# The first pair of a feed-forward layer takes both down units ahead of P4, and three of five layers make its T4 by an accumulating transfer

## What is computed

```python
def swiglu(x, w_gu, w_down):
    gate, up = jnp.split(x @ w_gu, 2, axis=-1)     # w_gu: 1024 x 5632
    return (jax.nn.silu(gate) * up) @ w_down       # w_down: 2816 x 1024
...
h = h + 0.5 * rmsnorm_2(swiglu(rmsnorm_2(h, g[0]), ffn_w_gu[l, 0], ffn_w_down[l, 0]), g[1])
```

## Time and profile before

| | us |
|---|---|
| median of 3 runs | 1264.8 (1263.88 to 1267.02) |
| the profiled execution | 1265.15 |
| its span, first to last instruction | 1263.4 |
| PE busy | 1249.7 (99%) |
| DVE busy | 1042.2 (82%) |
| ACT busy | 804.7 (64%) |
| POOL busy | 197.8 (16%) |

### The profile page before, as it was taken

How to read it: one execution, slowest core, us unless ns; L and a number is a source line. 1 busy time by engine, 2 the same in 40 slices (tenths; PEclk the granted TensorE clock), 3 DMA queues, 4 the chain that set the end, 5 groups by cost and what they waited for, 6 DMA issues and landing times.

```text
span 1263.4 us, 15541 instructions
## 1 busy us (share of the span) xinstructions
PE 1249.7 (99%) x5897; PEld 1029.2 (81%) x5897; DVE 1042.2 (82%) x1036; ACT 804.7 (64%) x988; POOL 197.8 (16%) x224
## 2 busy tenths in 40 slices
PE   9999999999999999999999999999999999999998
PEld 7888888888888888888878888888888877788886
DVE  6766689999799996767899997999977568899984
ACT  6674576666576664645666664766656467766662
POOL 6142130110001100202301101211001003301100
PEclk9999999999999999999999999999999999999999
DMA  9537498997649955568989978389745535999931
GB/s 335 175 101 229 128 327 251 267 273 250 199 147 253 272 172 187 194 223 213 334 242 247 265 248 260 123 240 274 219 167 179 180 125 170 321 287 263 266 133 44
DMA packets 143003, 277.32 MB, mean 220 GB/s; under 512 B 8993, under 2 KB 39897, under 8 KB 142929
## 3 DMA queue, kind: packets, MB, share of 16 engines
q1 hardware_dynamic: 120192, 229.67, 52.1%
q0 software_dynamic: 22288, 45.54, 19.7%
q10 hardware_dynamic: 448, 1.12, 0.2%
HBM read 275.24 MB, written 1.05 MB: 219 GB/s over the span
## 4 chain that ended last, share of the span: by engine, by line
PE 83%; DVE 8%; DMA 3%; issue 3%; ACT 2%; POOL 0%; SPq 0%; DVEq 0%; POOLq 0%; ACTq 0%
PE B L2115 15%; PE B L2117 15%; PE B L2116 15%; PE B L2571 7%; PE B L2573 7%; PE B L2572 7%; DVE w_lo L1366 5%; PE T L2115 3%; PE T L2117 3%; PE T L2116 3%; DMA Z<-in_ffn_w_gu 2%; DVE VD L1385 1%; ACT w_hi L1084 1%; PE T L2595 1%; DMA VD<-in_ffn_w_gu 1%
## 5 line engine op out<-in xcount | busy, mean ns | idle before, releaser
L1366 DVE TENSOR_TENSOR w_lo<-w_raw,w_hi 128x2048 fp32r<-128x2048 f32 x129 | 296.5, 2300 | 87.3 <-ACT w_hi L769 87.0
L769 ACT ACTIVATE w_hi<-w_raw 128x2048 fp32r<-128x2048 f32 x129 | 247.2, 1919 | 102.2 <-PE B L2573 59.7
L2115 PE MATMUL B<-w_hi,xt_lo 128*128 128x512 f32 x652 | 259.8, 398 | 2.4 <-DVE nat L2029 0.6
L2117 PE MATMUL B<-w_hi,xt_hi 128*128 128x512 f32 x652 | 254.5, 390 | 0.0
L2116 PE MATMUL B<-w_lo,xt_hi 128*128 128x512 f32 x652 | 254.1, 390 | 0.0
L2571 PE MATMUL B<-w_hi,act_lo 128*128 128x512 f32 x440 | 172.8, 393 | 0.8 <-DVE w_lo L1366 0.6
L2573 PE MATMUL B<-w_hi,act_hi 128*128 128x512 f32 x440 | 171.5, 390 | 0.0
L2572 PE MATMUL B<-w_lo,act_hi 128*128 128x512 f32 x440 | 171.3, 389 | 0.0
L2115 PEld LDWEIGHTS B<-w_hi,xt_lo 128*128 128x128 f32 x652 | 122.5, 188 | 31.5 <-issue 4.4
L2117 PEld LDWEIGHTS B<-w_hi,xt_hi 128*128 128x128 f32 x652 | 122.4, 188 | 26.1
L2116 PEld LDWEIGHTS B<-w_lo,xt_hi 128*128 128x128 f32 x652 | 122.6, 188 | 23.3
(11 more groups left out here) (331 smaller groups left out, 2115.9 us busy)
## 6 DMA issues: line engine op xcount, KB each, us to landing
w_raw<-in_ffn_w_down SPq DMA_DIRECT2D x88, 512.0 KB, 5.8
Z<-in_ffn_w_gu SPq DMA_DIRECT2D x64, 512.0 KB, 8.2
w_raw<-in_ffn_w_gu SPq DMA_DIRECT2D x48, 512.0 KB, 5.3
nat<-in_ffn_w_gu SPq DMA_DIRECT2D x32, 512.0 KB, 7.9
QT<-in_ffn_w_gu SPq DMA_DIRECT2D x32, 512.0 KB, 7.0
Z<-in_ffn_w_gu POOLq DMA_DIRECT2D x32, 512.0 KB, 9.1
w_raw<-in_conv_w_in SPq DMA_DIRECT2D x24, 512.0 KB, 4.8
w_raw<-in_w_down SPq DMA_DIRECT2D x22, 512.0 KB, 6.6
```

Source lines behind the costliest of these rows:

```text
L769: act.activation(whi[home(u)][:, :], raw[slot][:, :], ACT.Copy).then_inc(w_hi, 1)
L1366: dve.tensor_tensor(wlo[home(u)][:, :], src, whi[home(u)][:, :].bitcast(F32), ALU.subtract).then_inc(w_lo, 1)
L2115: pe.matmul(bank[:, :], lo[:, k, x], whi[s][:, c], start=first, stop=False, skip_group_check=more)
L2117: return pe.matmul(bank[:, :], hi[:, k, x], whi[s][:, c], start=False, stop=last, skip_group_check=more)
```

## The change

- `FFN_OPS` in pair 0: D0, D1, P4 instead of D0, P4, D1, on all engines that walk it.
- T4.0 in f = 1, 3, 4 (`FIRST_T4`) is made by an accumulating transfer that POOL issues after P6.0's low half; DVE's sum goes, and SP's refill of B21 no longer waits for it. In f = 0, 2 DVE still makes it, now after D0's low half.
- `act_out(1)` has the second pair of activation buffers and moves from the end of pair 0 to behind P3.0, on ACT and DVE.
- Sum T4.3 moves on DVE from behind P6.3 to behind act_out(7), ahead of P2.3.
- In f = 2 the sums T1.2 and T1.3 move on DVE from ahead of the down unit Db to behind C11.
- In SP's queue in pair 0, B12 is refilled ahead of B21.

```diff
-FFN_OPS += [(_n, 0) for _n in ("P1", "P2", "P5", "P6", "P3", "P7")] + [("D0", 0), ("P4", 0), ("D1", 0)]
+FFN_OPS += [(_n, 0) for _n in ("P1", "P2", "P5", "P6", "P3", "P7", "D0", "D1", "P4")]
...
 ADDED_T4 = (1, 2)
+FIRST_T4 = (1, 3, 4)
+def added_t4(f):
+    return ((0,) if f in FIRST_T4 else ()) + ADDED_T4
 def sums_of(f):
-    return (((0, "T1"), (0, "T2")) if f % 2 else ()) + ((0, "T4"),) + SUMS
+    return (((0, "T1"), (0, "T2")) if f % 2 else ()) + (() if f in FIRST_T4 else ((0, "T4"),)) + SUMS
...
         def act_parts(d):
-            return (ahi1, alo1) if is_second(d) else (ahi, alo)
+            return (ahi1, alo1) if d == 1 or is_second(d) else (ahi, alo)
... SP
-                        if name == "B21" and p == 0:
+                        if name == "B21" and p == 0 and f not in FIRST_T4:
                             sp.wait_ge(t_ok, sums_ready(f, 0, "T4"))
                 next_block("B22", "P3", 0)
+                next_block("B12", "P7", 0)
                 next_block("B21", "P2", 0)
-                next_block("B12", "P7", 0)
... POOL, add_blocks
+                if p0 and 0 in added_t4(f):
+                    add_block("T4", f, 0, w_gu)
                 for p in range(p0, SQUARES):
                     add_block("T3", f, p, w_gu)
-                    if p in ADDED_T4:
+                    if p in added_t4(f):
                         add_block("T4", f, p, w_gu)
... ACT
                 def act_out(d):
-                    if d == 1:
-                        act.wait_ge(w_used, u0 + OP["D0", 0] + 1)
                 block("P3", 0)
+                act_out(1)
                 keep("P5", 0)
                 block("P7", 0)
                 keep("P6", 0)
                 weights("D0")
+                weights("D1")
                 block("P4", 0)
-                weights("D1")
-                act_out(1)
... DVE
                 block("P3", 0)
-                weight_sum("T4", f, 0)
+                act_out(1)
                 block("P7", 0)
                 weights("D0")
-                block("P4", 0)
+                if f not in FIRST_T4:
+                    weight_sum("T4", f, 0)
                 result("C22", 0)
                 weights("D1")
                 result("C12", 0)
+                block("P4", 0)
+                result("C11", 0)
                 weight_sum("T1", f, 1)
-                act_out(1)
-                result("C11", 0)
                 for p in range(1, SQUARES):
...
-                    if p not in ADDED_T4:
-                        weight_sum("T4", f, p)
                     block("P3", p)
                     block("P7", p)
                     act_out(2 * p)
                     weights("Da", p - 1)
                     act_out(2 * p + 1)
+                    if p not in added_t4(f):
+                        weight_sum("T4", f, p)
                     block("P2", p)
                     result("C22", p)
                     block("P4", p)
                     result("C12", p)
-                    if p + 1 < SQUARES:
+                    if p + 1 < SQUARES and f != 2:
                         weight_sum("T1", f, p + 1)
                     weights("Db", p - 1)
                     result("C11", p)
+                    if p + 1 < SQUARES and f == 2:
+                        weight_sum("T1", f, p + 1)
... PE
                         down("D0")
+                        down("D1")
                     pe.wait_ge(c_ok, m + 1)
                     block("P4", p)
                     if p:
                         down("Db", p - 1)
-                    else:
-                        down("D1")
```

More of the change, by code:

```diff
@@ L79, in t4_added @@
 def t4_added(f, p):
-    return 32 * (len(ADDED_T4) * f + ADDED_T4.index(p) + 1)
+    return 32 * (sum(len(added_t4(g)) for g in range(f)) + added_t4(f).index(p) + 1)
 def down_block(name, p):
@@ L1078, in block @@
                         act.wait_ge(*((t1_in, 32 * f + 64) if src == "T1" else (t2_in, 16 * f + 32)))
-                    elif src == "T4" and p in ADDED_T4:
+                    elif src == "T4" and p in added_t4(f):
                         act.wait_ge(t4_in, t4_added(f, p))
```

## The result

The changed kernel takes 1275.4 us, median of 6 runs (1274.08 to 1276.89), against 1264.9 for the kernel before beside it (1263.88 to 1267.02): ratio 1.0077, 95% interval 1.0067 to 1.0088. The forecast was 1265.3, no change; it is 10.6 us slower. The profiled execution took 1276.89, with a span of 1275.1 and a granted clock of 0.999.

What follows compares the result with a forecast made beforehand. PE, busy 1249.7 of 1263.4 us, was the bound, so only its stalls could move. Layers f=0 to 4 at +0.68, -0.81, +2.08, -0.71, -0.71 gave +0.53: median 1265.3, own range 1263.5 to 1267.5, over all cases 1261.5 to 1268.0.

Steps and rivals of the forecast that it cites:

- The stall at P7.0: PE in pair 0: a stall of 0.41 and restart of about 0.1 go, 0.53 saved.
- P3.3's: Stall after pair 3's transposes goes as T4.3 moves: gain 0.68 in f=1 and f=2, 0.18 in f=0, 3, 4.
- The stalls of D1 and Db.1 in f=2: PE in f=2: 0.38 + 0.12 at D1 and 0.58 + 0.16 with restart 0.15 at Db.1 both go.
- The 23.15 chain of f=0 and f=2: Pair 0, D0's high half to P6.1 with DVE's late sum: P6.1 late, +0.86 in f=0, +0.37 in f=2.
- T1 behind Db: f=2, pairs 2 and 3: DVE and ACT chain 17.56 against PE's 16.32, P6 late, +2.68 in all.
- T3's lateness: f=2, T3 issued later behind the moved T1: 0.3 per pair, bounds 0 and 2.4.
- rival C: T3 late in f=2 by the full 2.4 per pair: +4.2, 1269.5; decides over 10.5 us from issue; chance 0.07.
- the three signs by which I would be wrong: P6.1 stalls in f=3 or f=4, T4.0 takes over 11 us, or P5.1 does not stall in f=0.
- The added transfer: T4.0 in f=1, 3, 4 lands 9.96 after issue, hidden; 0.15 put on f=1 for B12, bounds 0 and 1.5.
- 0.5 of cover and 0.09 of spare: Pair 0: T4.0 lands 0.5 before P4.0's high half must start; DVE's chain reaches P6.1 with 0.09 left.
- rival D: T4.0 lands late in f=1, 3, 4, sliding all to P6.1: 1.8 each, +5.4, 1270.7; chance 0.05.
- the lock rule: DVE and POOL share ports under an exclusive lock, so T4.0's issue could stand behind one more DVE step of 2.28.

Runs made afterwards that it cites:

- e4: The kernel before with only the sum T4.3 moved on DVE from behind P6.3 to ahead of P2.3, all layers: 1262.6 us, ratio 0.9983.
- e10: e4 with SP's refill of B22 behind that of B12 in every pair: 1263.7 us, ratio 0.9987.
- e7: The kernel before, SP's plain transfers after T3.2 and T3.3 also waiting for C11 (2.53 behind, not 1.93): 1264.9 us, ratio 1.0.
- e2: The changed kernel with the refill of B22 in pair 0 issued behind that of B12: 1271.1 us, ratio 1.0046.
- e11: e6 with the refill of B22 behind that of B12 in every pair: 1260.4 us, ratio 0.9963.
- e6: The changed kernel with T4.0 by transfer in all layers, pair 0's B22 behind B12, T1 ahead of Db, T1.1 ahead of P4.0: 1264.5 us, ratio 1.0.
- e12: The changed kernel with the sum T1.1 on DVE ahead of P4.0's low half and C11: 1280.8 us, ratio 1.0126.

## Why the prediction was wrong

**Right.** The stall at P7.0 goes in all layers. P3.3's goes, and the move pays 2.4 (e4) for 1.9. The stalls of D1 and Db.1 in f=2 go too, but that proves nothing: e4 and e10 keep D1 and T1 at their old places and have neither stall in f=2 (e4 has 0.99 at Db.1 in f=1 instead), and e7 has none at D1 and 0.15 at Db.1. I read 0.38 and 0.74 as the kernel's, and they were that one execution's. The 23.15 chain of f=0 and f=2 gives stalls of 0.52 and 0.69 or 0.81 with the restart, as forecast. T1 behind Db: the stalls of P5 and P6 in pairs 2 and 3 add to 2.9 for 2.68, and T3's lateness to 0.8 for 0.6 (it landed in 11.9 and 12.0, past the 10.5 at which rival C decides, at a fifth of C's price). The rows for these, steps back to back, were enough. Two of the three signs by which I would be wrong came: P6.1 stalls in f=3, and T4.0 takes over 11 us.

**The step that failed: "The added transfer".** I took one row, 9.96, as T4.0's duration, on the argument that pair 1's transfer "has the same size". What it does not have is the same neighbour. In the earlier trace rows SP's next plain transfer is issued 2.40 behind; for the new one it is 1.98 in f=1 and 2.05 in f=3, as P3.0's low half follows P6.0's at once, and SP refills B22 on it. It measured 12.67 and 12.26, and 10.12 in f=4 at 2.17. With only 0.5 of cover and 0.09 of spare behind, that is rival D, which I gave 0.05: it names the place and the slide to P6.1, at 1.8 a layer. The runs give 2.2 in f=1 and 1.7 in f=3 and nothing in f=4. So D's place came true and its cause did not. The text gave as cause the lock rule of the Trainium skill's page "SBUF — State Buffer", section "SBUF: two separate sides"; against DVE steps with two inputs, as here, the rule asks for a GpSimd operation that reads SBUF, and no trace shows POOL's issue to be one. It is 2.49 long, no longer than in the kernel before (2.43 to 2.50), and starts 0.3 after P6.0's low half is written. e2 shows another cause, since the same issue beside the same DVE steps lands in 8.8 once SP's transfer is moved. The longer landing was in the trace of before: T3 took "at most 13.7", and I used that row for T3 alone. Bounding T4.0 by it would have put D's 1270.7 in the range; 1275.4 would still have lain 4.7 beyond that, and the terms of the next paragraph cost 5.5.

**The terms that were put at nothing.** Of a step that is moved I counted DVE's and ACT's time, not what it does to the other added transfers: when they are issued and how far behind SP comes. Before, act_out(1) and C11 stood between the sum T1.1, which releases POOL's T3.1, and P1.1's low half, which releases SP's refill of B11. Both moved ahead, 0.60 each, and the distance went from 3.13 to 1.93, by just these 1.20. T3.1's landing goes from 10.0 to 10.2 (11.3 in f=0) up to 11.7 to 12.6 (in f=4 with five plain transfers in flight, so not by the distance alone). C11 now stands ahead of T1.1, and P4.0's low half has moved from ahead of C22 to between C12 and C11, so T3.1 is issued 1.0 to 3.1 later in the layer, which weighs as much as the landing. Together that costs 2.9; no run parts the two. The same once more: a chain of DVE without slack puts P3.1's low half at once behind P6.1's, so T4.1 has SP 1.93 behind it instead of 2.4, lands in 11.7 to 12.4 instead of 9.9 to 10.1 in f=0, 1 and 3, and costs 2.6. Of the 9.3 not forecast, e2 takes back 4.3 in the medians: T4.0's 3.9 and the 1.8 of Db.0 in f=1 and f=3, less what T3.1 and other waits cost more there. T4.1's cause is shown by e11 against e6: with B22 moved and nothing else it lands in 8.5 instead of 12.64 in f=1, and Db.0 doesn't stall. T3.1's waits go in e6 and e11 by the earlier issue alone, as it takes 13.7 to 15.0 there. e12 shows that T1.1's move without B22's moves the wait to T1.1.

**Left open.** Why the landing drops at a distance of about 2.06 is open: no run varies the distance finely at one place. At T3.1, how much is the distance's and how much the later issue's is open as well. The price of transfers in flight rests on e10's T3.1 alone, where the distance stayed at 3.13.

## What to carry to other kernels

A transfer's duration read from one row holds only with that row's neighbours: before moving or adding one, list what the other queues issue within 6 us of it and what is in flight. Take the longest like row as the bound when the cover is under 1 us. Moving a short step between two releases changes when another queue issues and how far behind the next queue comes, and that can cost more than the step. Put the plain refill whose reader comes last behind the one that is needed first, and keep it at least 2.1 us, better 4.5 us, behind an added transfer (table below). Look then at who gets the moved refill in flight beside it: in e10 the same move gained nothing.

## What the runs showed of the hardware

All 13 traces together, an added transfer of 1 MB in two halves, issued by POOL in 2.4 to 2.5 us, with at most three plain transfers in flight; time from issue to both landed:

| SP's next issue behind it | transfers | landed after, us: least, median, most |
|---|---|---|
| 1.8 to 2.05 | 180 | 11.2, 12.0, 13.8 |
| 2.08 to 2.5 | 68 | 9.5, 10.1, 11.6 |
| 2.5 to 3.2 | 57 | 9.5, 10.0, 12.2 |
| over 4.5 | 56 | 8.4, 8.7, 9.6 |

The first half takes 5.7 to 6.8 in all of these: it is the second that is held up. POOL is still issuing it when SP's transfer starts in the first row and in 60 of the 68 of the second, so that alone does not part the two rows. Left out are T3.0 of f=2 in the 13 traces, with SP 0.02 behind: there the first half is late too (8.2 to 10.4). With five or six in flight at the issue, 57 transfers at any distance, the first half takes 7.6 to 12.4 and both 11.0 to 16.5. In which part of the chip the halves are held is not shown. The Trainium skill's page "DMA: Bandwidth & Descriptors", section "Queues, rings and completion order", has each DMA engine take turns between its queue rows, a packet at a time; that fits a half that lands in 8.0 when the plain transfer is issued late and in 11.9 when it is issued early, as in e2 and after. It does not tell why 0.1 us of distance is worth 2 us.
